# The end of the expert mixture in a diffusion step: the sum so far goes through TensorE into the banks of the last pair

## The reference, cut to what matters

```python
def expert_choice_ffn(h, w_router, w_gate, w_up, w_down):
    ...
    xe = jax.vmap(lambda hb, ib: hb[ib])(h, idx)
    a = jnp.einsum('becd,edf->becf', xe, w_gate)
    u = jnp.einsum('becd,edf->becf', xe, w_up)
    ye = jnp.einsum('becf,efd->becd', jax.nn.silu(a) * u, w_down) * gate[..., None].astype(h.dtype)
    return jax.vmap(lambda yb, ib: jnp.zeros((n, d), yb.dtype).at[ib.reshape(-1)].add(yb.reshape(-1, d)))(ye, idx)

for i in range(DEPTH):
    ...
    fp = expert_choice_ffn(hp, moe_w_router[i], moe_w_gate[i], moe_w_up[i], moe_w_down[i])
    fs = expert_choice_ffn(hs, moe_w_router[i], moe_w_gate[i], moe_w_up[i], moe_w_down[i])
    xp = xp + rms_norm(fp, norm_post[i, 1]) * g2_p
    xs = xs + rms_norm(fs, norm_post[i, 1]) * g2_s
```

## Time and profile before

| | |
|---|---|
| time, median of 3 runs | 2401.84 us (2399.01 to 2402.60) |
| the profiled execution | 2398.12 us |
| its span | 2396.3 us |
| mean granted TensorE clock | 0.975 of full |
| busy share TensorE / VectorE / ScalarE / GpSimd | 94% / 73% / 53% / 8% |
| share of the chain that ended last, by engine | TensorE 89%, VectorE 5%, ScalarE 4% |

### The profile page before, as it was taken

How to read it: one execution, slowest core, us unless ns; L and a number is a source line. 1 busy time by engine, 2 the same in 40 slices (tenths; PEclk the granted TensorE clock), 3 DMA queues, 4 the chain that set the end, 5 groups by cost and what they waited for, 6 DMA issues and landing times.

```text
span 2396.3 us, 27235 instructions
## 1 busy us (share of the span) xinstructions
PE 2263.3 (94%) x10016; PEld 1552.0 (65%) x10016; DVE 1757.9 (73%) x1948; ACT 1272.0 (53%) x1347; POOL 194.6 (8%) x226
## 2 busy tenths in 40 slices
PE   6999999999988999999999798997989999999995
PEld 2866868768654666666666455876746666666663
DVE  2675675756767898999999544454378989999996
ACT  3321312212235777887777434444357777877773
POOL 1000000000022000111000110000120001110001
PEclk9999999999999999999999899998999999999997
DMA  7443434425435999999999310101169999999991
GB/s 269 123 141 96 151 123 134 155 82 175 131 145 205 339 361 356 359 361 341 347 337 362 113 38 1 36 1 37 60 233 348 356 346 362 366 338 350 339 354 61
DMA packets 167652, 529.15 MB, mean 221 GB/s; under 512 B 13525, under 2 KB 22282, under 8 KB 167306
## 3 DMA queue, kind: packets, MB, share of 16 engines
q1 hardware_dynamic: 162954, 515.35, 59.8%
q0 software_dynamic: 2304, 8.39, 1.0%
q10 hardware_dynamic: 2304, 4.20, 0.5%
HBM read 516.72 MB, written 11.17 MB: 220 GB/s over the span
## 4 chain that ended last, share of the span: by engine, by line
PE 89%; DVE 5%; ACT 4%; issue 1%; POOL 1%; DMA 0%; SPq 0%; ACTq 0%; POOLq 0%; DVEq 0%
PE ps L1725 85%; PE ps L1728 4%; POOL SMALL L607 0%; POOL SMALL L606 0%; ACT W_HI L337 0%; DVE IDX L1426 0%; DVE B L1252 0%; DVE X L1253 0%; DVE WO_LO L1611 0%; DVE MIXREG L1425 0%; DMA REGION<-in_ada_b_dram 0%; ACT W L337 0%; DVE B L1227 0%; ACT WO_HI L337 0%; DVE ROUTE L1428 0%
## 5 line engine op out<-in xcount | busy, mean ns | idle before, releaser
L1463 DVE TENSOR_TENSOR W_LO<-RAW_W,W_HI 128x2048 fp32r<-128x2048 f32 x384 | 867.4, 2287 | 76.2 <-ACT W_HI L337 72.7
L337 ACT ACTIVATE W_HI<-RAW_W 128x2048 fp32r<-128x2048 f32 x384 | 726.4, 1916 | 193.2 <-PE ps L1725 192.2
L1725 PE MATMUL ps<-W_HI,XET_HI 128*80 128x512 f32 x1024 | 322.3, 396 | 7.4 <-DVE B L1497 5.8
L1725 PE MATMUL ps<-W_HI,XET_LO 128*80 128x512 f32 x1024 | 319.5, 393 | 0.0
L1725 PE MATMUL ps<-W_LO,XET_HI 128*80 128x512 f32 x1024 | 319.3, 393 | 0.0
L1725 PEld LDWEIGHTS ps<-W_HI,XET_HI 128*80 128x80 f32 x1024 | 151.0, 149 | 89.0 <-DVE B L1497 6.7
L1725 PEld LDWEIGHTS ps<-W_LO,XET_HI 128*80 128x80 f32 x1024 | 151.9, 148 | 85.7 <-issue 0.9
L1725 PEld LDWEIGHTS ps<-W_HI,XET_LO 128*80 128x80 f32 x1024 | 151.7, 148 | 84.5 <-issue 0.7
L1196 DVE SCALAR_TENSOR_TENSOR ADA_SUM<-ADA_RAW,NCOL,ADA_SUM 128x512 f32<-128x512 f32 x280 | 191.2, 745 | 0.3 <-DMA ADA_RAW<-in_ada_w_dram 0.3
L1725 PE MATMUL ps<-W_HI,HTE_HI 128*80 128x512 f32 x512 | 166.8, 407 | 8.6 <-issue 8.6
L1725 PE MATMUL ps<-W_LO,HTE_HI 128*80 128x512 f32 x512 | 161.2, 396 | 0.0
(11 more groups left out here) (270 smaller groups left out, 3511.7 us busy)
## 6 DMA issues: line engine op xcount, KB each, us to landing
RAW_W<-in_moe_w_gate_dram SPq DMA_DIRECT2D x128, 1024.0 KB, 5.9
RAW_W<-in_moe_w_up_dram SPq DMA_DIRECT2D x128, 1024.0 KB, 5.7
RAW_W<-in_moe_w_down_dram SPq DMA_DIRECT2D x128, 1024.0 KB, 5.4
ADA_RAW<-in_ada_w_dram SPq DMA_DIRECT2D x80, 512.0 KB, 3.6
RING_RAW<-in_ret_w_in_dram SPq DMA_DIRECT2D x48, 512.0 KB, 4.6
W<-in_ada_w_dram SPq DMA_DIRECT2D x4, 2048.0 KB, 14.1
RING_RAW<-in_ret_w_out_dram SPq DMA_DIRECT2D x16, 512.0 KB, 4.7
xn_rows<-B SPq DMA_DIRECT2D x8, 512.0 KB, 13.4
```

What stands on the lines that cost most here:

```text
L337: return nc.scalar.activation(out, in_, ACT.Copy, scale=scale)
L1463: V_.tensor_tensor(W_LO[:, slot], RAW_W[:, slot], W_HI[:, (place + i) % HSLOTS].bitcast(F32), ALU.subtract).then_inc(MS_["lo"], 1)
L1725: return T.matmul(out, lhsT, rhs, start=first, stop=last)
```

## The change

In both mixtures the last pair is no longer added to the sum by VectorE.

- TensorE first multiplies the sum so far, `YB2`, by the identity into the tile's two banks (`so_far`: two plain fp32 products of 128x512), and `combine` then accumulates its four products on top without clearing. The products of tiles 0 and 1 stand ahead of the wait for `YE_LO`; those of tiles 2 and 3 stand between the combines.
- The five additions of VectorE (`last_rows`) are gone. ScalarE's squares and VectorE's L1252 read the tile from PSUM.
- The banks are now 6, 0, 2, 4 and, for the prompt, 2 again. So the prompt's part (`last_prompt`) waits until the update of tile 2 is done (`x_ready`). In the second mixture it stands at the end of TensorE's program. In the first mixture it stands in `mla_pe`, between `latents(0, 0)` and the transposes of tile 1.
- Because the banks stay in use until the updates have read them, the norm's transposes of the second layer use bank 6 for every tile, the latents use banks 0 and 4 instead of 2 and 0, and `latents(0, 0)` waits for the update of tile 1 and `latents(1, 0)` for that of tile 3.

```diff
-        LAST_BANK = (6, 0, 2, 6, 0)
+        LAST_BANK = (6, 0, 2, 4, 2)
-        NORM_BANK = (4, 4, 4, 0)
+        NORM_BANK = ((4, 6, 4, 6, 4), (4, 6, 4, 6, 4), (6, 6, 6, 6, 6), (0, 2, 0, 2, 0))
...
                 def squares(t):
-                    update_squares(n, t, YB2, B1[:, t % NT, :], *((MS_["c_ev"], b["c_ev"] + 4 * (PAIRS - 1) + t + 1) if t < NLAT else (MS_["cp_ev"], b["cp_ev"] + PAIRS // 2)))
+
+                    if t < NT:
+                        rows = ps[:, LAST_BANK[t]:LAST_BANK[t] + 2, :].rearrange("p a n -> p (a n)")
+                        update_squares(n, t, rows, B1[:, t % NT, :], *((MS_["c_mm"], b["c_mm"] + 4 * (PAIRS - 1) + t + 1) if t < NLAT else (MS_["cp_mm"], b["cp_mm"] + PAIRS // 2)))
...
-                    chain.link(V_.scalar_tensor_tensor(Y[:, t, :], Y[:, t, :], RSTDU[:, t:t + 1], GATE[:, t // NLAT, :], ALU.mult, ALU.mult))
+                    rows = Y[:, t, :] if bank is None else ps[:, bank[t]:bank[t] + 2, :].rearrange("p a n -> p (a n)")
+                    chain.link(V_.scalar_tensor_tensor(Y[:, t, :], rows, RSTDU[:, t:t + 1], GATE[:, t // NLAT, :], ALU.mult, ALU.mult))
...
-                last_rows(0)
-                last_rows(1)
-                update(n, 0, YB2)
+                update(n, 0, YB2, LAST_BANK)
                 for t in range(NT):
-                    last_rows(t + 2)
                     if not layer:
                         normalise(n + 1, t)
-                    update(n, t + 1, YB2)
+                    update(n, t + 1, YB2, LAST_BANK)
                     if not layer:
                         norm_dve_tile(n + 1, 1, 0, t)
...
+                def so_far(t):
+
+                    for half in range(2):
+                        mm(ps[:, LAST_BANK[t] + half, :], IDENT[:], YB2[:, t, half * HALF:(half + 1) * HALF], True, False)
...
                 pe.wait_ge(gate_ev, 4 * (2 * layer + 2))
+                pe.wait_ge(MS_["c_ev"], b["c_ev"] + 4 * (PAIRS - 1))
+                for t in range(2):
+                    so_far(t)
                 for t in range(NLAT):
-                    combine(PAIRS - 1, t, LAST_BANK[t], 0 if t < 3 else 1)
-                combine_prompt(PAIRS - 1, PAIRS // 2 - 1, LAST_BANK[NLAT], 2)
+                    if t >= 2:
+                        so_far(t)
+                    combine(PAIRS - 1, t, LAST_BANK[t], 0, False)
+
+                def last_prompt():
+
+                    pe.wait_ge(MS_["cp_ev"], b["cp_ev"] + PAIRS // 2 - 1)
+                    pe.wait_ge(x_ready, NT * (2 * layer + 1) + 3)
+                    so_far(NLAT)
+                    combine_prompt(PAIRS - 1, PAIRS // 2 - 1, LAST_BANK[NLAT], 0, False)
+
+                return last_prompt
...
-                        last = mm(ps[:, 2 * ((t + 1) % 2) + n, 0:hi - lo], normed(2, k, t), WIN2[k // 4][:, k % 4, lo:hi], k == 0, k == KD - 1)
+                        last = mm(ps[:, 4 * (t % 2) + n, 0:hi - lo], normed(2, k, t), WIN2[k // 4][:, k % 4, lo:hi], k == 0, k == KD - 1)
...
-                        pe.wait_ge(*((MS_["cp_ev"], PAIRS // 2) if t else (MS_["c_ev"], 4 * PAIRS - 1)))
+                        pe.wait_ge(x_ready, NT + (4 if t else 2))
                     tokens_normed(2, t + 1)
                     latents(t, 0)
                     if t == 0:
-                        pe.wait_ge(MS_["c_ev"], 4 * PAIRS)
+                        last_prompt()
                     if t + 1 < NT:
                         norm_pe_tile(2, t + 1)
                     latents(t, 1).then_inc(MA["lat_mm"], 1)
```

More of the change, by code:

```diff
@@ L749, in norm_act_tile @@
                 for k in range(4, 8):
-                    last = nc.scalar.activation(normed(n, k, t), ps[:, NORM_BANK[n] + 1 + 2 * (t % 2), (k - 4) * P:(k - 3) * P],
+                    last = nc.scalar.activation(normed(n, k, t), ps[:, NORM_BANK[n][t] + 1, (k - 4) * P:(k - 3) * P],
                                                 ACT.Identity, scale=scale_col(layer, sub, k, c), bias=shift_col(layer, sub, k, c))
@@ L761, in gates_act, with update_squares @@
                     act_copy(GATE[:, j // 2, (j % 2) * HALF:(j % 2 + 1) * HALF], ps[:, j, :]).then_inc(gate_ev, 1)
-            def update_squares(n, t, Y, squares, ready, needs):
+            def update_squares(n, t, rows, squares, ready, needs):
                 if 0 <= t < NT:
@@ L768, in update_squares @@
                         act.wait_ge(ru_ss, NT * n + t)
-                    nc.scalar.activation(squares, Y[:, t, :], ACT.Square, accum_out=SSU[:, t:t + 1]).then_inc(ru_ss, 1)
+                    nc.scalar.activation(squares, rows, ACT.Square, accum_out=SSU[:, t:t + 1]).then_inc(ru_ss, 1)
             for t in range(NT):
@@ L882, in latent_rows @@
                 act.wait_ge(MA["lat_mm"], t + 1)
-                b = 2 * ((t + 1) % 2)
+                b = 4 * (t % 2)
                 act_copy(LATN[:, t, :], ps[:, b:b + 2, :].rearrange("p a n -> p (a n)")[:, 0:WIN]).then_inc(MA["lat_ev"], 1)
@@ L1121, in mla_act @@
                             norm_act_tile(3, 1, 1, 2)
-                    update_squares(2, t, B1, squares, MA["mo_ev"], 2 * (t + 1))
+                    update_squares(2, t, B1[:, t, :], squares, MA["mo_ev"], 2 * (t + 1))
                     if t >= 2:
@@ L1226, in norm_dve_tile @@
                 for k in range(4):
-                    last = V_.tensor_scalar(normed(n, k, t), ps[:, NORM_BANK[n] + 2 * (t % 2), k * P:(k + 1) * P],
+                    last = V_.tensor_scalar(normed(n, k, t), ps[:, NORM_BANK[n][t], k * P:(k + 1) * P],
                                             scale_col(layer, sub, k, c), shift_col(layer, sub, k, c), ALU.mult, ALU.add)
@@ L1244, in gates_dve, with update @@
                     last.then_inc(gate_diag, 1)
-            def update(n, t, Y):
+            def update(n, t, Y, bank=None):
                 if 0 <= t < NT:
@@ L1768, in norm_pe_tile @@
                 for k in range(KD):
-                    last = tr(ps[:, NORM_BANK[n] + 2 * (t % 2) + k // 4, (k % 4) * P:(k % 4 + 1) * P], B1[:, t, k * P:(k + 1) * P])
+                    last = tr(ps[:, NORM_BANK[n][t] + k // 4, (k % 4) * P:(k % 4 + 1) * P], B1[:, t, k * P:(k + 1) * P])
                     if k % 4 == 3:
@@ L2060, in hidden_tr, with combine @@
                             last.then_inc(MS_["t_mm"], 1)
-                def combine(pair, t, bank, emptied):
+                def so_far(t):
+                    for half in range(2):
+                        mm(ps[:, LAST_BANK[t] + half, :], IDENT[:], YB2[:, t, half * HALF:(half + 1) * HALF], True, False)
+                def combine(pair, t, bank, emptied, fresh=True):
                     if t == 0:
@@ L2070, in combine, with combine_prompt @@
                         for i, y in enumerate((YE_HI, YE_LO)):
-                            last = mm(ps[:, bank + half, :], CT[:, t, :], y[:, half * HALF:(half + 1) * HALF], i == 0, i == 1)
+                            last = mm(ps[:, bank + half, :], CT[:, t, :], y[:, half * HALF:(half + 1) * HALF], fresh and i == 0, i == 1)
                     last.then_inc(MS_["c_mm"], 1)
-                def combine_prompt(pair, quad, bank, emptied):
+                def combine_prompt(pair, quad, bank, emptied, fresh=True):
                     pe.wait_ge(MS_["ctp"], b["ctp"] + quad + 1)
                     pe.wait_ge(MS_["y_ev"], b["y_ev"] + 2 * (pair + 1))
-                    pe.wait_ge(MS_["c_ev"], b["c_ev"] + 4 * pair + emptied)
+                    if emptied:
+                        pe.wait_ge(MS_["c_ev"], b["c_ev"] + 4 * pair + emptied)
                     for half in range(2):
-                        last = mm(ps[:, bank + half, :], CTP[:], YEP[:, half * HALF:(half + 1) * HALF], True, True)
+                        last = mm(ps[:, bank + half, :], CTP[:], YEP[:, half * HALF:(half + 1) * HALF], fresh, True)
                     last.then_inc(MS_["cp_mm"], 1)
@@ L2153, in mix_pe, with mla_pe @@
                 pe.wait_ge(gate_ev, 4 * (2 * layer + 2))
+                pe.wait_ge(MS_["c_ev"], b["c_ev"] + 4 * (PAIRS - 1))
+                for t in range(2):
+                    so_far(t)
                 for t in range(NLAT):
-                    combine(PAIRS - 1, t, LAST_BANK[t], 0 if t < 3 else 1)
-                combine_prompt(PAIRS - 1, PAIRS // 2 - 1, LAST_BANK[NLAT], 2)
-            def mla_pe():
+                    if t >= 2:
[7 more added lines that the diff above has]
+                return last_prompt
+            def mla_pe(last_prompt):
                 base = [16 * n for n in BEFORE_MLA]
@@ L2345, in _ @@
             if STAGE >= 2:
-                mix_pe(0)
+                last_prompt = mix_pe(0)
             if STAGE >= 3:
-                mla_pe()
-                mix_pe(1)
+                mla_pe(last_prompt)
+                mix_pe(1)()
 _INS = ["x_prompt", "x_sample", "state_ret_fwd", "state_ret_bwd", "cache_mla_ckv", "cache_mla_krope", "c", "c_ctx",
```

9 lines of the change are left out of this document (2 added, 7 removed).

## The result

After the change the median of 12 runs is 2406.05 us (2401.03 to 2407.28), against 2402.12 us (2397.19 to 2403.63) for 12 runs of the kernel before on the same chip. The ratio is 1.0018, with a 95% interval of 1.0010 to 1.0026: slower by 3.9 us, between 2.4 and 6.2, which lies within the 0.2% that I called about the limit of the measurement. I had predicted 2404.6 us.

A forecast was written before the change was run, and what follows sets the result against it. TensorE was taken to bound most of the span, so only its pauses at both mixtures' ends mattered; +3.34 - 0.5 = +2.8 us on the median 2401.84 gave 2404.6 us, range 2400.0 to 2408.4.

The forecast's parts named there:

- The front: Start of both mixtures' ends: `so_far` hidden by the wait for `YE_LO`, first square 1.85 and 1.74 us earlier.
- the rival in which the clock falls before it: Both fronts: low clock makes `so_far` take 6.88 us, each mixture loses 3.2 us; +9.2, 2411 us; chance 0.05.
- No price for PSUM: Squares and L1252 in both mixtures: reading PSUM takes as long as SBUF; square bounds -0.04 and +0.04 us.
- That rival: Square or L1252 slower from PSUM, eating the addition's 1.24 us; some +5 us, chance 0.03.
- `latents(0, 0)`: First mixture: its 16 records start 1.85 us earlier and keep 9.47 us, partly at low clock, instead of 6.88.
- The prompt in the stream: First mixture: `last_prompt` stands in TensorE's unbroken stream and costs 1.72 + 1.72 = 3.44 us.
- The stall before `latents(1, 0)`: First mixture: TensorE, ready after 3.45 us, waits for tile 3's update until 5.20 us; stall 1.75 us.
- the third rival: The 1.75 us stall in the first mixture lowers the clock, another 2.0 us; +4.8, 2406.6 us; chance 0.13.
- The first two: Rivals: neither tail cost (stall, last prompt's low clock) comes, 2400.0 us, chance 0.07; one missing, 2402.6 to 2402.9, chance 0.2.
- The cache load: First mixture: SyncE's load, queued behind the prompt's combine, moves from 1361.90 to about 1382 and costs nothing.
- First mixture in sum: Front, prompt and stall of the first mixture: -1.85 + 3.44 + 1.75 = +3.34 us, carried to the end.
- Second mixture: VectorE's pace 2.45 us a tile, TensorE hole 3.6 us, low clock +2.0 at the prompt; sum -0.5 us.

The follow-up runs named there:

- the second: The changed kernel timed once more against the kernel before, on another chip than the first comparison: 2405.28 us, ratio 1.0015 (1.0006 to 1.0024).
- before's second profile: The kernel before, unchanged, profiled again for the stages' scatter: one run of 2404.18 us, middle 949.16 us.
- the kernel with all three edits: Changed kernel plus second prompt in tile 0's banks, first prompt back in TensorE's pause, tile 3's update moved ahead: 2391.11 us, ratio 0.9960 against the kernel before.

## Why the prediction held, step by step

- **The front.** Forecast -1.85 and -1.74 us. From the first product of a combine to the first L1256 it is 3.42 and 3.41 us (1355.64 to 1359.06; 2379.84 to 2383.25) against 5.08 and 4.98: -1.66 and -1.57. The first square follows 1.21 us after the first product, not 1.11; to the latents in the first mixture it came to -1.81, counted from the first product (15.82 us in the earlier trace rows, 14.01 after). `so_far` took its 3.44 us under the wait for `YE_LO`, and the rival in which the clock falls before it is refuted: the combines run at the fast pitch.
- **No price for PSUM.** The square from PSUM takes 1.00 to 1.03 us, L1256 1.27 to 1.28, against 1.06 and 1.27 to 1.29 from SBUF. That rival falls too.
- **`latents(0, 0)`.** I kept 9.47 us. It took 8.90 (1369.65 to 1378.55), 0.57 less. This is the mis-sized term of the first mixture. I had carried over one execution's share of the lower clock; the row of these 16 records is 7.03 to 9.64 us long in the profiles here.
- **The prompt in the stream.** Forecast +3.44; 1378.55 to 1381.98 is 3.43, and leaving out half of it gave back 1.75 us.
- **The stall before `latents(1, 0)`.** Forecast 1.75. By the forecast's own 3.45 us behind the transposes TensorE was ready at 1385.43 and started at 1387.15: 1.72. Moving the update gave back 1.81. The latents behind it ran 7.13 us, so a pause of 1.53 us did not lower the clock here, and the third rival falls. The first two fall as well, since this pause and the low clock at the last prompt both came.
- **The cache load.** It moved to 1382.17, as forecast, and its first reader stands 5.01 us behind the first gate product in both kernels: no cost.
- **First mixture in sum:** forecast +3.34, measured +2.84.
- **Second mixture.** Pace 2.46 us a tile for 2.45, hole 3.63 us for 3.6, the low clock +1.76 for +2.0 (2390.85 to 2396.21 is 5.36 us, against 3.60 at full speed), sum -0.58 for -0.5. That the sum is this close is partly luck: the front fell 0.17 short and the low clock cost 0.24 less, and the two nearly cancel. My +1.0 for 1.2 GHz throughout should have been +0.9. The rule of the Trainium skill, "SBUF — State Buffer", section "Who interferes with whom", agrees with the rows: under L1256, with one operand in PSUM, L607 took 0.55 us (2383.86), beside L1257, with two inputs in SBUF, 1.58 us at 1385.92 in the first mixture.
- **What I had no term for.** Ends of +2.26 us are just under the interval of the first comparison (2.4 to 6.2) and inside that of the second (1.4 to 5.8). The forecast of +2.8 stands between the ends and the runs' +3.9, and some 1.6 us of the latter are in neither end. One of my own signs of being wrong, a stage far from both ends that changes its length, appeared in the first two profiles (945.34 and 949.65), and before's second profile (949.16) takes away its force without settling it. The two profiles of before fit the two groups of its timed runs: 2398.12 us with the short middle, 2404.18 with the long one. After's runs lie almost all in one group, which suggests that the long middle comes more often after the change; no run shows it, since the timed runs have no marks, and it stays open.

## What to carry to other kernels

An addition that is moved from an idle-waiting engine onto the matrix engine is free only where that engine waits; count for each product whether it stands in a pause or in the unbroken stream, and what the buffers that it fills must wait for. Here the same change with other banks for one tile, one update moved ahead, and one product back in a pause went from 3 to 4 us slower to some 10 us faster, of which the two ends hold 4.9. Look also at what a pause does to the work behind it: filling it with products that nobody needs paid 1.65 us where they fitted, and cost 1.36 where they were twice too long.

## What the runs showed that I had not expected

- A low-clock spell moves with the work. Taking the prompt out of the stream into the pause put the spell onto the prompt (3.63 us for four records) and took it off the latents (9.06 to 7.13). With the update moved ahead too it covered both (3.78 and 9.35).
- Among three pauses of 1.5, 1.4 and 1.3 us with little work between them the clock fell in the second (0.70 from 1366 to 1367) and stood at 0.50 up to 1376 in the kernel with all three edits; in the one with only the prompt moved the low stretch was shorter, and behind a single pause of 1.53 us, in a long stream, there was none. With one of the three filled and one shortened to 0.7 us the clock stayed at 1.00.
- The same kernel has a stretch of 10 us at 0.92 in one execution and at 0.56 in another. It cost 2.5 us there, as much as the change did in its two ends together.
